# Third attention of a three-attention block chain: another order of its groups, its first scores inside the input product, its output product between groups

## The reference, cut to what matters

```python
z = h @ w_in                        # 1024 -> 1840: q, three (k, v) pairs, gates
q, kv_c, kv_s, kv_w, g = split(z)   # 16 query heads, 2 key/value heads, 64 wide
gates = sigmoid(g + gate_b)         # three a head
k_cmp, v_cmp = [silu(blocks(kv_c[i]) @ w1[i]) @ w2[i] for i in (k, v)]   # 15 compressed keys
# per block of 128 queries:
o_c = softmax(q @ k_cmp, where the block has ended) @ v_cmp
o_s = causal_softmax(q @ k_s) @ v_s    # 256 tokens: every block of keys is selected
o_w = causal_softmax(q @ k_w) @ v_w    # window 512: all of them
y = (gates[0] * o_c + gates[1] * o_s + gates[2] * o_w) @ w_out
```

## Time and profile before

| | |
|---|---|
| median of 3 runs | 1512.7 us (1512.33 to 1513.07) |
| profiled execution | 1518.84 us, its span 1517.1 us |
| TensorE busy | 1459.4 us (96%) |
| VectorE, ScalarE, GpSimd busy | 1055.5 (70%), 729.8 (48%), 77.3 us (5%) |
| mean granted TensorE clock | 0.986 |
| third attention with its input product | about 1157 to 1307 us |

### The profile page before, as it was taken

One profiled execution on the slowest core, in us unless ns is written; L12 is line 12 of the kernel. 1 busy time (PEld: TensorE's weight loads), 2 busy tenths in 40 slices (PEclk: granted clock), 3 DMA queues, 4 the chain that ended last, 5 costly groups with the idle time before them and its releaser, 6 DMA issues.

```text
span 1517.1 us, 18745 instructions
## 1 busy us (share of the span) xinstructions
PE 1459.4 (96%) x7206; PEld 1199.5 (79%) x7206; DVE 1055.5 (70%) x1432; ACT 729.8 (48%) x1104; POOL 77.3 (5%) x133
## 2 busy tenths in 40 slices
PE   8998999999999999998899999999999989999998
PEld 7885777888887888888778888788888767788886
DVE  5797565886777777766487777877677678675544
ACT  6544544544355434364554334544345765554342
POOL 7200100000000000010000000000000000000000
PEclk9998999999999999999899999999999999899999
DMA  8861434687856978634368878587883610566560
GB/s 299 281 240 38 141 137 165 224 297 256 279 193 222 319 247 279 240 118 142 100 237 302 287 258 284 175 304 268 281 286 127 215 42 1 181 193 201 188 208 28
DMA packets 189087, 314.21 MB, mean 207 GB/s; under 512 B 6896, under 2 KB 100440, under 8 KB 189000
## 3 DMA queue, kind: packets, MB, share of 16 engines
q1 hardware_dynamic: 148800, 232.87, 46.2%
q10 hardware_dynamic: 38408, 75.65, 13.8%
q0 software_dynamic: 1792, 4.51, 0.9%
HBM read 311.92 MB, written 1.07 MB: 206 GB/s over the span
## 4 chain that ended last, share of the span: by engine, by line
PE 81%; DVE 8%; ACT 5%; POOL 3%; issue 2%; DMA 1%; POOLq 0%; ACTq 0%; DVEq 0%
PE ps L1167 24%; PE ps L1169 23%; PE ps L1168 23%; PE ps L1176 5%; PE ps L1496 2%; PE ps L1314 2%; PE ps L1442 1%; DVE wlo L1123 1%; DVE rmax L2331 1%; ACT whi L1104 1%; ACT sp L1860 1%; DVE tmp L2015 1%; POOL sp L2648 0%; DMA raw<-in_nsa_w_out 0%; DMA w2s<-in_nsa_cmp_w 0%
## 5 line engine op out<-in xcount | busy, mean ns | idle before, releaser
L1123 DVE TENSOR_TENSOR wlo<-raw,whi 128x2048 fp32r<-128x2048 f32 (+2 forms) x168 | 381.5, 2274 | 109.6 <-ACT whi L1104 109.3
L1167 PE MATMUL ps<-whi,aT 128*128 128x512 f32 (+3 forms) x1000 | 399.8, 400 | 7.0 <-DVE aTl L2003 4.0
L1169 PE MATMUL ps<-wlo,aT 128*128 128x512 f32 (+3 forms) x1000 | 388.4, 388 | 0.0
L1168 PE MATMUL ps<-whi,aTl 128*128 128x512 f32 (+3 forms) x1000 | 387.1, 387 | 0.0
L1104 ACT ACTIVATE whi<-raw 128x2048 fp32r<-128x2048 f32 (+2 forms) x166 | 314.1, 1896 | 35.5 <-PE ps L1169 28.0
L1167 PEld LDWEIGHTS ps<-whi,aT 128*128 128x128 f32 x1000 | 188.4, 188 | 50.4 <-issue 10.2
L1169 PEld LDWEIGHTS ps<-wlo,aT 128*128 128x128 f32 x1000 | 188.0, 188 | 39.6
L1168 PEld LDWEIGHTS ps<-whi,aTl 128*128 128x128 f32 x1000 | 188.7, 189 | 34.1
L1802 ACT ACTIVATE hT<-ps 128x256 fp32r<-128x256 f32 (+1 forms) x102 | 42.2, 413 | 342.3 <-PE ps L1176 342.3
L1167 PE MATMUL ps<-whi,hT 128*128 128x512 f32 (+1 forms) x364 | 141.2, 390 | 1.4 <-ACT z L1777 1.4
L1169 PE MATMUL ps<-wlo,hT 128*128 128x512 f32 (+1 forms) x364 | 138.4, 382 | 0.0
(11 more groups left out here) (271 smaller groups left out, 2047.8 us busy)
## 6 DMA issues: line engine op xcount, KB each, us to landing
raw<-in_ff_w SPq DMA_DIRECT2D x176, 512.0 KB, 4.9
raw<-in_ff_w SPq DMA_DIRECT2D x44, 1024.0 KB, 5.2
qT<-in_ada_w ACTq DMA_DIRECT2D x36, 1024.0 KB, 6.6
pT<-in_ada_w ACTq DMA_DIRECT2D x36, 1024.0 KB, 7.5
raw<-in_w_up SPq DMA_DIRECT2D x16, 1024.0 KB, 6.0
raw<-in_w_down SPq DMA_DIRECT2D x16, 1024.0 KB, 5.6
raw<-in_w_in SPq DMA_DIRECT2D x9, 1024.0 KB, 9.7
raw<-in_w_ckv SPq DMA_DIRECT2D x8, 1024.0 KB, 5.5
```

The source lines that it names most:

```text
L1123: dve.tensor_tensor(lo_of(u), raw_of(u), hi_of(u).bitcast(F32), ALU.subtract).then_inc(w_lo, 1)
L1167: pe.matmul(out_ap, hi, w, start=start, stop=False)
L1168: pe.matmul(out_ap, lo, w, start=False, stop=False)
L1169: return pe.matmul(out_ap, hi, wl, start=False, stop=stop)
```

## The change

The window keys and the gathering are nested behind unit 4 instead of 3. Behind unit 6 stand the turn of the queries of heads 0 to 7, the compression's first product, and a head of the attention: scores of groups 0 and 1 on TensorE, maximum and exponentials of group 0 on the others. The turn of the hidden rows stands behind unit 7. The queries of heads 8 to 15 are turned in the attention's step 1, the compressed keys and values are made in step 4, with the gate; groups 4 and 8 wait for them (late). The order of the groups is now: first branch, the heads 0 to 7 ahead of the others, then the four compressed groups, then the second branch. One group in four has its causal mask made on TensorE. The output's first columns are turned in step 19, and the first output slab is made in two halves, in steps 20 and 21.

```diff
--- before.py
+++ after.py
@@ -339,7 +339,7 @@
         r = self.rounds(n, who)
-        self.keys_turned = r[-2:]
+        self.keys_turned = r
@@ -571,10 +571,19 @@
+    heads = {}
+
+    def attend_head(which, turned, ahead):
+
+        heads[which] = dict(groups=attention_groups(p, which), ahead=ahead)
+        p.stage("attend_head", which=which, turned=list(turned), **heads[which])
+
-    def attend(which, turned, w, gate, nest, k0=0):
-        groups = attention_groups(p, which)
+    def attend(which, turned, w, gate, nest, k0=0, late=None):
+        head = heads.get(which, dict(ahead=0))
+        groups = head.get("groups") or attention_groups(p, which)
...
+                head=which in heads, ahead=head["ahead"], late=late)
@@ -690,28 +699,39 @@
             def turn_hid():
                 r = p.rounds(2, "D")
                 p.stage("cmp_turn", rounds=r, hid=list(r_cmp))
+                r_cmp[:] = r
+
+            def hidden_then_head():
                 p.turned("q_nsa", 2, ["A", "D"], c0=0)
                 turned.extend(p.keys_turned)
-                r_cmp[:] = r
+                hidden()
+                attend_head("nsa", turned, 1)
+
+            late = {}
+
+            def turn_q_rest():
+                p.turned("q_nsa", 2, ["A", "D"], c0=512)
+                late[4] = p.keys_turned
 
             def cmp_out():
                 r = p.rounds(2, "D")
                 p.stage("cmp_out", rounds=r, turned=list(r_cmp))
-                p.turned("q_nsa", 2, ["A", "D"], c0=512)
-                turned.extend(r + p.keys_turned)
+                late[8] = r
+                p.gate(layer, 5)
...
-                     inner={2: keys, 3: rows, 5: hidden, 6: turn_hid, 7: cmp_out})
+                     inner={2: keys, 4: rows, 6: hidden_then_head, 7: turn_hid})
             def finish():
-                p.o_turn(0, "nsa", 10)
-                early(0)()
+                p.o_turn(0, "nsa", 8)
 
             def finish_rest():
-                p.o_turn(4, "nsa", 12)
+                p.o_turn_tiles(4, "nsa", 12)
                 early(1)()
 
-            attend("nsa", turned, A["nsa_w_out_2"][0], (p.n_gates + 1, 1.0), {2: lambda: p.gate(layer, 5), 21: finish, 22: finish_rest})
+            attend("nsa", turned, A["nsa_w_out_2"][0], (p.n_gates + 1, 1.0),
+                   {1: turn_q_rest, 4: cmp_out, 19: finish, 20: early(0, 0), 21: early(0, 1), 22: finish_rest}, late=late)
@@ -736,12 +756,14 @@
         for br in (0, 1):
-            spec += [dict(kind="nsa", br=br, t=t, h0=h, nh=4) for t in range(NT) for h in (0, 4, 8, 12)]
-        spec += [dict(kind="cmp", t=t, h0=h, nh=8) for h in (0, 8) for t in range(NT)]
+            if br:
+                spec += [dict(kind="cmp", t=t, h0=h, nh=8) for h in (0, 8) for t in range(NT)]
+            spec += [dict(kind="nsa", br=br, t=t, h0=h + h2, nh=4) for h in (0, 8) for t in range(NT) for h2 in (0, 4)]
+        spec[1]["second"] = True
...
-        g["psum"] = g["kind"] in ("swa", "diff", "mla", "cross")
+        g["psum"] = g["kind"] in ("swa", "diff", "mla", "cross") or g["kind"] == "nsa" and g["t"] == 1 and g["h0"] % 8 == 0
@@ -966,10 +988,12 @@
-        third = {"swa": z[:, 0, 768:1792], "diff": z[:, 0, 768:1792], "mla": zc[:, 1, 1024:2048]}
+        third = {"swa": z[:, 0, 768:1792], "diff": z[:, 0, 768:1792], "mla": zc[:, 1, 1024:2048], "cross": z[:, 0, 1024:2048]}
...
             n = g["g"] % 3
+            if n == 2 and g.get("second"):
+                return gbc[:, :]
@@ -1407,7 +1431,10 @@
-                def scores(g):
+                def scores(i):
+                    g = gs[i]
+                    for t in (st.get("late") or {}).get(i, ()):
+                        wait_emptied(pe, T, lambda j: t)
@@ -1440,10 +1467,10 @@
-                                                 start=True, stop=kind == "nsa")
+                                                 start=True, stop=not g["psum"])
...
-                                elif kind != "nsa":
+                                elif g["psum"]:
                                     last = masked(sv[:, 2 * i:2 * i + 2, nk - P:nk], causal_r[:, :])
@@ -1497,10 +1524,14 @@
-                scores(gs[0])
+                if not st.get("head"):
+                    scores(0)
+                if st["kind"] == "attend_head":
+                    scores(1)
+                    return
                 for i in range(len(gs) + 3):
-                    if i + 1 < len(gs):
-                        scores(gs[i + 1])
+                    if i + 1 < len(gs) and not (i == 0 and st["head"]):
+                        scores(i + 1)
@@ -1871,8 +1902,12 @@
                 act.wait_ge(t_ready, st["turned"][-1] + 1)
+                if st["kind"] == "attend_head":
+                    for g in gs[0:st["ahead"]]:
+                        exps(g)
+                    return
                 for i in range(len(gs) + 3):
-                    if i < len(gs):
+                    if st["ahead"] <= i < len(gs):
                         exps(gs[i])
@@ -2404,8 +2439,12 @@
                 dve.wait_ge(t_ready, st["turned"][-1] + 1)
+                if st["kind"] == "attend_head":
+                    for g in gs[0:st["ahead"]]:
+                        smax(g, None)
+                    return
                 for i in range(len(gs) + 3):
-                    if i < len(gs):
+                    if st["ahead"] <= i < len(gs):
                         smax(gs[i], gs[i - 3] if i >= 3 else None)
```

More of the change, by code:

```diff
@@ L572, in make_plan @@
     out = []
-    def attend(which, turned, w, gate, nest, k0=0):
-        groups = attention_groups(p, which)
+    heads = {}
[5 more added lines that the diff above has]
+        groups = head.get("groups") or attention_groups(p, which)
         out[:] = [dict(p.out_begin(w, gate, k0), half=groups[len(groups) // 2 - 1])]
-        p.stage("attend", which=which, turned=turned, groups=groups, nest=attention_turns(p, groups, nest))
+        p.stage("attend", which=which, turned=turned, groups=groups, nest=attention_turns(p, groups, nest),
+                head=which in heads, ahead=head["ahead"], late=late)
     def first_half(n=None):
@@ L1574, in _ @@
                          q_mla=turns_of, k_mla=turns_of, q_nsa=turns_of, k_nsa=turns_of, w_nsa=turns_of,
-                         o_T=turns_of, attend=attend, out_first=out_first, out_rest=out_rest, cmp_hid=cmp_hid, cmp_turn=cmp_turn, cmp_out=cmp_out)
+                         o_T=turns_of, attend=attend, attend_head=attend, out_first=out_first, out_rest=out_rest, cmp_hid=cmp_hid, cmp_turn=cmp_turn, cmp_out=cmp_out)
             for st in p.stages:
@@ L1925, in _ @@
                          q_mla=turns_of, k_mla=turns_of, q_nsa=turns_of, k_nsa=turns_of, w_nsa=turns_of, o_T=o_T,
-                         attend=attend, conv=conv, cmp_rows=cmp_rows, cmp_hid=cmp_hid,
+                         attend=attend, attend_head=attend, conv=conv, cmp_rows=cmp_rows, cmp_hid=cmp_hid,
                          out_first=out_first, out_rest=out_rest)
@@ L2538, in _ @@
                          q_mla=turns_of, k_mla=turns_of, q_nsa=turns_of, k_nsa=turns_of, w_nsa=turns_of, o_T=o_T,
-                         attend=attend, diff_sums=diff_sums, diff_scale=diff_scale, conv=conv, conv_taps=conv_taps, out_first=out_first,
+                         attend=attend, attend_head=attend, diff_sums=diff_sums, diff_scale=diff_scale, conv=conv, conv_taps=conv_taps, out_first=out_first,
                          out_rest=out_rest, cmp_rows=cmp_rows, cmp_hid=cmp_hid,
```

## The result

The changed kernel takes 1524.8 us in the median of ten executions (1521.1 to 1527.8), the kernel before 1513.2 beside it; the ratio is 1.0070, 95% interval 1.0058 to 1.0082. So it is slower by 0.7%, which is 10.6 us (the two medians differ by 11.6; the ratio and its interval are used from here on), where no difference was forecast (1512.2) and the range ended at 1517.0. The profiled execution took 1527.79 us, its span 1526.0.

What follows compares the result with a forecast made beforehand. TensorE was taken as the bound, 81% of what ends last. Its losses were summed as 8.8 + 7.9 + 2.6 + 1.0 = 20.3 us against 20.8 before, 0.5 less, so 1512.2 us, range 1505.5 to 1517.0.

Steps and rivals of the forecast that it cites:

- The 1.4 us gap goes, as the copy of z has a unit of 5.5 us to finish: Input product, window keys: moving them one unit later removes TensorE's 1.4 us gap.
- on TensorE at 1213.0: Input product with all that is in it ends on TensorE at 1213.0, against 1213.4 before.
- VectorE's wait for the compressed keys: Middle of the attention: VectorE reaches the copies of the compressed keys before TensorE has made them and stands 3.7 us.
- Bank emptied after the second group's exponentials: Attention's start: query turns wait 3.0 us for a bank ScalarE empties only after the second group's exponentials.
- Middle: Third attention, with compressed groups and compression output in the middle: TensorE loses 7.9 us where 0 to 0.5 was lost.
- End: Before the last values, with the output product between groups: 0.9 and 1.7 us left, 2.6 in all.
- the bank of the hidden rows: Attention's start: turning the first probabilities waits 2.7 us for the PSUM bank that the hidden rows' copies empty.
- where the end phase lost 9.9: End phase of the kernel before: gaps of 6.0 and half clock of 3.9 us, against 2.6 lost after the change.
- With 0.4 for a stretch of half clock: Input product and attention's start: 0.4 us for half clock in the idle microseconds, within 8.8 lost there.
- A: Whole stretch: losses are exchanged, as worked out in the forecast; by itself 1509.7 to 1515.7; chance 0.50.
- B: Middle groups: no queue builds up, so 3 us is lost instead of 7.9, giving 1505.8; chance 0.30.
- C: Output product: the clock falls once more there and costs 4.5 us, giving 1516.7, slower; chance 0.20.

Runs made afterwards that it cites:

- the second profile of before: The kernel before, unchanged, profiled again: ratio 1.0004; this profiled execution took 1511.5 us, with 122.4 us from the keys' turn behind unit 2 to the second output slab.
- the old input and the new middle: Changed kernel with the input product and nesting of the kernel before and no head, all other parts of the change kept: ratio 1.0018, 2.7 us slower than before.
- the output product behind: Changed kernel with the output turns and whole first output slab behind the groups, as before: ratio 1.0107, 5.6 us slower than the changed kernel.
- shift: Kernel before with only window keys moved behind unit 4, compression product behind unit 6, and its rows' turn, queries 0 to 7 and compression output behind unit 7: ratio 1.0036.
- heads first: Kernel before with only the order of the sixteen masked groups changed, heads 0 to 7 of both query tiles first in each branch: ratio 1.0054, 8.2 us slower.
- compressed in the middle: Kernel before with only the four compressed groups moved from the end to between the two branches: ratio 1.0031, 4.7 us slower.
- tail and masks: Kernel before with the output product between the last groups and one 256-key group in two masked on TensorE: ratio 0.9992.
- the masks on VectorE: Changed kernel with all sixteen masked groups masked by VectorE's addition again: ratio 1.0108, 5.7 us slower than the changed kernel.
- the compression early again: Changed kernel with window keys behind unit 3 and the compression's first product behind unit 5 again; query turns and head stay behind unit 6: ratio 1.0018.
- the gathering later: Changed kernel with the gathering of the rows to be compressed, with the sigmoid, behind unit 5 instead of unit 4: ratio 1.0050.

## Why the prediction was wrong

**The step that failed first** is "The 1.4 us gap goes, as the copy of z has a unit of 5.5 us to finish", with the sum for the input product that ends "on TensorE at 1213.0". I asked what waits for the copies of z at the window keys, and not what else does: the first product of every block waits for its output bank. The wait did not go, it moved to unit 4 (1.05), and a larger one came at unit 6 (3.89), with 3.4 us of half clock behind it (eight slots of 0.43 for 0.23, 1.6). The input product with all that is in it ended at 1220.46; less the 1.5 that this execution was late from the start, that is 5.9 after the 1213.0 of the sum. I had ScalarE's string of 7.0 us in hand and moved it on paper by one unit, and rightly: its end was forecast at 1194.3 and stands at 1196.10, less the 1.5 again. I followed it to the next split and to the load of the output weight, not to the copy that stands behind it. Undone, it gives 7.9 us; that was not among the rivals.

**The terms of the sum that held.** VectorE's wait for the compressed keys: forecast 3.7, this row:

```profile
1240.78 0.73 DVE L2561 COPY kcz<-ps 64x15 f32<-64x15 f32 x4 [3.67 <-PE ps L1593]
```

Bank emptied after the second group's exponentials: 3.0, measured 2.68. Middle: 0.6 and 0.6, measured 0.40 and 0.42; 0.1 and 1.2, measured 0.27 and 0.81; 0.5 and 1.9, measured 0.48 and 1.84; 0.9 and 2.0, measured 0.91 and 1.85; values of the third group 0.7, measured 0.63. End: 0.9 and 1.7, measured 0.75 and 1.44. A group with two mask products takes 0.23 us more (1.95 for 1.72), 0.9 in all, forecast 1.0. Two terms were too large: the bank of the hidden rows, 2.7, measured 0.83, because TensorE came later by the new wait and found VectorE nearly done; and the fifth group's scores, 1.3, measured 0.3. (The terms listed for the middle add up to 7.8, not 7.9, unless the 0.1 of a held bank is counted apart.)

**The second step that failed** is the end phase, "where the end phase lost 9.9". 3.9 of it was half clock, and the second profile of before has none there. I took one execution's fall for the kernel's. In the profile of 122.4 the kernel before loses 17.9 in the stage, not 20.8. By my own terms after, 20.3, the change should have been slower than that one by 2.4 us. So even with the input product right, the forecast could have been at the edge of slower; the run with the old input and the new middle measured 2.7.

**The third** is that waits were priced at their own length. "With 0.4 for a stretch of half clock" stands against 1.4 there, 3.3 behind the fifteenth group's values (6.8 us at half clock: from these values to the next it takes 7.9 us, and 4.6 in the first profile with the output product behind, at full clock), and 1.6 at unit 6. Over 16 executions the changed kernel spends 40 us at half clock, the kernel before 31. These 9 us are 2.7 of the 10.6 at 0.30 each, and 4.5 at most; the rest is waits and the mask products. TensorE's waits in the stage sum to 18.7 us after, and to 12.6 and 12.9 in the two profiles of before.

**The rivals.** A, the losses are exchanged: the mechanism is what the waits show, the size fell. B, the middle holds no queue: refuted, 25.57 busy of 29 us, and 4.7 us for its place alone. C had the sign, not the place: the clock is 1.00 in the output product (1302 to 1311) and fell elsewhere, the last time from 1281.5 to 1288.3, where I had named "no half clock from 1287 on" as a sign. So C's "slower" came true by luck: the fall is not in the place that it named, and the wait at unit 6 is not in it. The masks on TensorE are worth 5.7 us to the changed kernel, with 12 to 16 us less at half clock. No run isolates VectorE's fixed time with its source in PSUM. The Trainium skill ("TensorE: Matmul & The Clock Gate", Part 1) calls half rate the default that activity lifts. The falls behind the waits at unit 6 and at the fifteenth group's values agree; the 13.7 us above began behind waits too, but stayed at half clock with TensorE busy throughout, which does not fit the rule in its plain form.

**The parts do not add.** Alone on the kernel before: shift 5.4, heads first 8.2, compressed in the middle 4.7, tail and masks -1.2 together. In the changed kernel the masks and the tail take back 5.7 and 5.6, though alone they give next to nothing. For the masks nearly all of it is clock, for the tail about half is clock and half waits, as the sums above say; why the clock needs them in the new order and not in the old one is not shown. The whole is 10.6.

## What to carry to other kernels

When a stage is moved along a product, look for each unit whose output bank it needs, who empties that bank, and what now stands ahead of the copy on that engine; the work that filled the time may be the very stage that was moved. Do not enter a half-clock stretch of one profile into a ledger as the kernel's: work out the mean over the executions from span and clock, and price a new wait with the chance of a fall behind it. An order in which long and short groups take turns can cost more than any wait it removes; try it alone.

## What was not expected of the hardware

Most waits made by program order repeat to 0.01 us from one execution to the next, but whether the clock falls behind a wait of some 1 us need not. In the two profiles of the changed kernel both repeat, falls too. In those of the kernel before, where the falls differ, waits near them differ as well: the first turn of probabilities waits 1.71 us in one and 2.60 in the other. In the order with heads first, one execution ran the 29 us from the last masked groups to the output product at 1.00 and another at 0.53, after the same wait (1.07 and 1.06). A fall can last with TensorE busy in every microsecond of it: 13.70 of 13.70 at 0.50 with the masks on VectorE, and as long at the same groups in the runs with the compression early again and with the gathering later. What decides between the two was not found; that part stays open.
